# The last FFN round by thirds of the tokens

## What is computed

```python
def _conv_ffn(h, conv_prev, P):
    u = h @ P['ffn_w_up']                       # 1024 -> 5632
    ext = jnp.concatenate([conv_prev.astype(u.dtype), u], axis=1)
    z = P['ffn_conv_b']
    for j in range(CONV_WIDTH):                 # 3 taps over the tokens
        z = z + ext[:, j:j + T] * P['ffn_conv_w'][j]
    za, zb = jnp.split(z, 2, axis=-1)
    return (jax.nn.silu(za) * zb) @ P['ffn_w_down'], ext[:, T:]
...
    ff, conv_T = _conv_ffn(h2, conv0, P)
    x = x + g2 * _rmsnorm(ff, P['norm_post_ffn'])
```

## Time and profile before

| | us |
|---|---|
| median of 3 runs (lowest, highest) | 1694.37 (1692.67, 1698.76) |
| the profiled execution: its time | 1695.05 |
| the profiled execution: its span, first to last instruction | 1693.2 |
| busy in the span: TensorE matmul, VectorE, ScalarE, GpSimd | 1476.3, 827.7, 534.2, 112.1 |

### The profile page before, as it was taken

The page is one execution under the profiler, slowest core; times in us unless marked ns, Lnnn a source line. Parts: engine busy times, 40 slices in busy tenths (PEclk is TensorE's granted clock), DMA queues, the critical chain, the costliest instruction groups (busy, mean ns, idle before and its releaser), DMA issues.

```text
span 1693.2 us, 28608 instructions
## 1 busy us (share of the span) xinstructions
PE 1476.3 (87%) x12458; PEld 1377.8 (81%) x12458; DVE 827.7 (49%) x985; ACT 534.2 (32%) x677; POOL 112.1 (7%) x172
## 2 busy tenths in 40 slices
PE   4799998776688997679839999999999999999972
PEld 1799998543587897459728999999999999999972
DVE  3742333663566557361086544545455444554446
ACT  3311211555345532242244232322312313223232
POOL 0000000000202110022221000000000000000013
PEclk7899999887799999789979999999999999999987
DMA  8341111541000000212121111111111111111022
GB/s 337 106 113 51 51 38 53 176 149 51 1 3 3 3 12 26 77 38 113 38 112 54 43 63 37 50 38 46 52 37 50 51 48 50 37 37 62 25 110 100
DMA packets 30994, 107.52 MB, mean 64 GB/s; under 512 B 5352, under 2 KB 8184, under 8 KB 29872
## 3 DMA queue, kind: packets, MB, share of 16 engines
q1 hardware_dynamic: 30912, 106.30, 18.0%
HBM read 93.29 MB, written 11.40 MB: 62 GB/s over the span
## 4 chain that ended last, share of the span: by engine, by line
PE 76%; DVE 14%; ACT 5%; DMA 2%; issue 2%; SPq 1%; DVEq 0%; POOL 0%; ACTq 0%
PE ps L496 47%; PE ps L900 12%; PE ps L646 6%; DMA raw<-ada 2%; PE ps L477 2%; DVE Z L1831 2%; PE ps L628 1%; PE ps L543 1%; PE ps L558 1%; PE ps L750 1%; PE ps L748 1%; PE ps L572 1%; DVE acc L1865 1%; PE ps L769 1%; SPq L336 1%
## 5 line engine op out<-in xcount | busy, mean ns | idle before, releaser
L496 PE MATMUL ps<-XS,spl 128*128 128x344 f32 x5184 | 824.1, 321 | 38.2 <-DVE XS L1794 20.7
L496 PEld LDWEIGHTS ps<-XS,spl 128*128 128x128 f32 x5184 | 819.5, 189 | 41.8 <-issue 25.2
L900 PE MATMUL ps<-act,spl 128*128 128x344 f32 x1584 | 255.8, 322 | 9.8 <-DVE act L1843 9.0
L900 PEld LDWEIGHTS ps<-act,spl 128*128 128x128 f32 x1584 | 251.7, 190 | 12.6 <-issue 9.3
L1831 DVE SCALAR_TENSOR_TENSOR Z<-U,par,Z 128x1023 f32<-128x1023 f32 x88 | 112.9, 1283 | 162.1 <-ACT Z L1249 156.5
L1865 DVE TENSOR_TENSOR acc<-acc,ps 128x1032 f32<-128x1032 f32 x88 | 108.2, 1229 | 128.6 <-PE ps L900 128.5
L1231 ACT ACTIVATE spl<-raw 128x1024 fp32r<-128x1024 f32 x66 | 68.4, 1054 | 284.1 <-PE ps L900 198.4
L1422 DVE TENSOR_TENSOR spl<-raw,spl 128x1024 fp32r<-128x1024 f32 x28 | 34.2, 1225 | 169.6 <-ACT spl L972 169.5
L1784 DVE TENSOR_TENSOR spl<-raw,spl 128x1024 fp32r<-128x1024 f32 x66 | 79.6, 1222 | 61.3 <-ACT spl L1231 60.1
L972 ACT ACTIVATE spl<-raw 128x1024 fp32r<-128x1024 f32 x28 | 29.6, 1060 | 210.8 <-PE ps L496 210.8
L1246 ACT ACTIVATE U<-ps 128x1032 f32<-128x1032 f32 x44 | 45.3, 1029 | 160.2 <-PE ps L496 158.5
(11 more groups left out here) (280 smaller groups left out, 1568.8 us busy)
## 6 DMA issues: line engine op xcount, KB each, us to landing
raw<-ada SPq DMA_DIRECT2D x48, 512.0 KB, 5.1
raw<-up SPq DMA_DIRECT2D x44, 512.0 KB, 3.3
raw<-down SPq DMA_DIRECT2D x22, 512.0 KB, 3.4
raw<-w_in SPq DMA_DIRECT2D x20, 512.0 KB, 3.4
xT<-xT SPq DMA_DIRECT2D x4, 1032.0 KB, 11.5
X<-xT SPq DMA_DIRECT2D x1, 4128.0 KB, 13.0
x_dram<-X SPq DMA_DIRECT2D x8, 516.0 KB, 2.6
X<-x_dram SPq DMA_DIRECT2D x1, 4128.0 KB, 12.7
```

The costliest lines, as they stand in the source:

```text
L496: mm = nc.tensor.matmul(ps[:, 3 * bank_set + t, 0:SL], w[:, a, k * P:(k + 1) * P], x[:, k, b, t * SL:(t + 1) * SL], start=(k == order[0] a ...
L900: mm = nc.tensor.matmul(ps[:, 3 * (down_set(i, y)) + t, 0:SL], w[:, a, k * P:(k + 1) * P], act2[:, f, b, t * SL:(t + 1) * SL], start=(f == ...
```

## The change

The last round of the FFN is taken apart along the tokens, in three thirds of 344.

- TensorE: round 10 is written out after a loop over nine. Its last up product is made third by third, each with all 24 matmuls into a bank of its own. The last round's down products go by third t and chunk k, six matmuls each (`TAIL`, 24 products) into the banks 0 to 3 in turn. The total of the squares of a third (`tail_total`, two matmuls) stands behind product (t + 1, 3), the last at the end.
- ScalarE: Silu of the first half at once, then for each third two evacuations and the high part; then a square for each product, and `tail_root(t)` behind the square of product (t + 1, 3) or at the end. The root stays in PSUM (banks 6 and 7).
- VectorE: taps, gate and low part for the three thirds one after the other, then an add for each product. Scaling, gate and residual are two operations for a chunk of a third (`tail_norm`): the first multiplies acc by gate and root into PSUM, the second adds X1. Those of the first third stand behind the adds (1, 5) to (2, 4), the first three of the second behind (2, 5) to (2, 7), the others at the end. GpSimd scales nothing any more and sums the squares of each third.
- SP: a third of X1 is loaded into a buffer of its own ahead of the loop over the rounds, the other two where all of X1 was loaded; 24 stores of a third of a chunk replace 8 of a chunk.

```diff
+(X1a,), at2 = place([("X1a", [P, KD, SL], F32)], at2)
...
+THIRDS = [slice(t * SL, t * SL + SL) for t in range(3)]
+TAIL = [(t, k) for t in range(3) for k in range(KD)]
+def tail_square(n):
+    return (Z, U)[n % 12 // 6][:, n % 6 // 3, THIRDS[n % 3]]
...
+sp.wait_ge(s("x1_out"), 16 * KD)
+dma(X1a[:], x1_dram[:, :, THIRDS[0]], s("x1a_in"))
...
-sp.wait_ge(s("x1_out"), 16 * KD)
 sp.wait_ge(s("ffn_mm"), JOBS - KD)
-dma(X1[:], x1_dram, s("x1_in"))
+dma(X1[:, :, THIRDS[1]], x1_dram[:, :, THIRDS[1]], s("x1b_in"))
+dma(X1[:, :, THIRDS[2]], x1_dram[:, :, THIRDS[2]], s("x1c_in"))
...
-for k in range(KD):
-    sp.wait_ge(s("y_ready"), k + 1)
-    dma(io["o_y"][:, k], acc[:, k], s("y_out"))
-sp.wait_ge(s("y_out"), 16 * KD)
+for n, (t, k) in enumerate(TAIL):
+    sp.wait_ge(s("y_ready"), n + 1)
+    dma(io["o_y"][:, k, THIRDS[t]], acc[:, k, THIRDS[t]], s("y_out"))
+sp.wait_ge(s("y_out"), 16 * len(TAIL))
...
+round_of(LAST - 1)
+pe.wait_ge(s("w3_lo"), (LAST - 1) * 6 + 4)
+pe.wait_ge(s("up_out"), (LAST - 1) * 4 + 2)
+for t in range(3):
+    for k in range(KD):
+        for n, (a, b) in enumerate(((0, 0), (0, 1), (1, 0))):
+            mm = nc.tensor.matmul(ps[:, 3 + t, 0:SL], spl3[:, 0, a, k * P:(k + 1) * P], XS[:, k, b, THIRDS[t]],
+                                  start=(k == 0 and n == 0), stop=(k == KD - 1 and n == 2))
+    if t < 2:
+        mm.then_inc(s("up_third"), 1)
+mm.then_inc(s("ffn_mm"), 1)
+def tail_total(t):
+    pe.wait_ge(s("sq_added"), (KD - 1) * (t + 2))
+    if t == 2:
+        pe.wait_ge(s("y_ready"), KD)
+    nc.tensor.matmul(ps[:, 6 + t % 2, 0:SL], ones, sqF[:, THIRDS[t]], start=True, stop=False)
+    pe.wait_ge(s("sq_c"), 2 * KD + KD * (t + 1))
+    nc.tensor.matmul(ps[:, 6 + t % 2, 0:SL], ones, tail_square(KD * t + KD - 1), start=False, stop=True
+                     ).then_inc(s("sq_total"), 1)
+pe.wait_ge(s("w3_lo"), 3 * FC)
+pe.wait_ge(s("g_lo"), FC - 1)
+for n, (t, k) in enumerate(TAIL):
+    if n >= 4:
+        pe.wait_ge(s("tail_out"), n - 3)
+    elif n == 3:
+        pe.wait_ge(s("third_out"), 1)
+    else:
+        pe.wait_ge(s("up_out"), 4 * LAST - 1)
+    for f in range(2):
+        if k == 0 and f == 1:
+            pe.wait_ge(s("lo_third"), t + 1)
+        for m, (a, b) in enumerate(((0, 0), (0, 1), (1, 0))):
+            mm = nc.tensor.matmul(ps[:, n % 4, 0:SL], spl3[:, 1 + f, a, k * P:(k + 1) * P], act2[:, f, b, THIRDS[t]],
+                                  start=(f == 0 and m == 0), stop=(f == 1 and m == 2))
+    mm.then_inc(s("tail_mm"), 1)
+    if t >= 1 and k == 3:
+        tail_total(t - 1)
+tail_total(2)
...
+act.wait_ge(s("conv_done"), 2 * FC - 1)
+nc.scalar.activation(Z[:, 0], Z[:, 0], ACT.Silu).then_inc(s("silu_done"), 1)
+act.wait_ge(s("g_done"), FC)
+for t in range(3):
+    if t < 2:
+        act.wait_ge(s("up_third"), t + 1)
+    else:
+        act.wait_ge(s("ffn_mm"), JOBS - KD)
+    nc.scalar.activation(U[:, 1, THIRDS[t]], ps[:, 3 + t, 0:SL], ACT.Copy)
+    nc.scalar.activation(Z[:, 1, THIRDS[t]], ps[:, 3 + t, 0:SL], ACT.Identity,
+                         bias=col(PARAM_AT["ffn_conv_b"][0], 2 * FC - 1),
+                         scale=col(PARAM_AT["ffn_conv_w"][0] + 2 * 2 * FC, 2 * FC - 1)).then_inc(s("third_out"), 1)
+    act.wait_ge(s("g_third"), t + 1)
+    nc.scalar.activation(act2[:, 1, 0, THIRDS[t]], G[:, THIRDS[t]], ACT.Copy).then_inc(s("hi_third"), 1)
+def tail_root(t):
+    act.wait_ge(s("sq_total"), t + 2)
+    inverse_root(ps[:, 6 + t % 2, 0:SL], ps[:, 6 + t % 2, 0:SL], eps[:, 0:1], 1.0 / D).then_inc(s("std2"), 1)
+for n, (t, k) in enumerate(TAIL):
+    act.wait_ge(s("tail_out"), n + 1)
+    if n >= 12:
+        t0, k0 = TAIL[n - 12]
+        if k0 < KD - 1:
+            act.wait_ge(s("sq_added"), (KD - 1) * (t0 + 1) + k0 + 1)
+        else:
+            act.wait_ge(s("sq_total"), t0 + 2)
+    nc.scalar.activation(tail_square(n), acc[:, k, THIRDS[t]], ACT.Square).then_inc(s("sq_c"), 1)
+    if t >= 1 and k == 3:
+        tail_root(t - 1)
+tail_root(2)
...
+def tail_sum(t, k):
+    total = sqF[:, THIRDS[t]]
+    pool.wait_ge(s("sq_c"), 2 * KD + KD * t + k + 1)
+    if k == 0:
+        nc.gpsimd.tensor_copy(total, tail_square(KD * t)).then_inc(s("sq_added"), 1)
+    else:
+        pool.wait_ge(s("sq_added"), (KD - 1) * (t + 1) + k)
+        nc.gpsimd.tensor_tensor(total, total, tail_square(KD * t + k), ALU.add).then_inc(s("sq_added"), 1)
+for t, k in TAIL:
+    if k < KD - 1:
+        tail_sum(t, k)
...
-add_down(FC // 2, True)
-dve.wait_ge(s("std2"), 3)
-dve.wait_ge(s("x1_in"), 16)
-dve.wait_ge(s("down_out"), KD * (FC // 2))
-out, x1 = acc[:, :, T:N], X1[:, :, T:N]
...
+z, u = Z[:, 1], U[:, 1]
+for t in range(3):
+    dve.wait_ge(s("third_out"), t + 1)
+    for n in (1, 0):
+        d = CW - 1 - n
+        a, b = max(t * SL, d), min(t * SL + SL, T)
+        link(nc.vector.scalar_tensor_tensor(z[:, a:b], u[:, a - d:b - d],
+                                            col(PARAM_AT["ffn_conv_w"][0] + n * 2 * FC, 2 * FC - 1), z[:, a:b],
+                                            ALU.mult, ALU.add))
+    if t == 2:
+        link(nc.vector.tensor_copy(at_chunk(ftail, 2 * FC - 1), u[:, T - 2:N]))
+        nc.vector.tensor_tensor(z[:, T:N], z[:, T:N], at_chunk(conv_add, 2 * FC - 1), ALU.add
+                                ).then_inc(s("conv_done"), 1)
+        dve.wait_ge(s("conv_done"), 2 * FC)
+    dve.wait_ge(s("silu_done"), FC)
+    nc.vector.tensor_tensor(G[:, THIRDS[t]], Z[:, 0, THIRDS[t]], z[:, THIRDS[t]], ALU.mult).then_inc(s("g_third"), 1)
+    dve.wait_ge(s("hi_third"), t + 1)
+    nc.vector.tensor_tensor(act2[:, 1, 1, THIRDS[t]], G[:, THIRDS[t]], act2[:, 1, 0, THIRDS[t]].bitcast(F32),
+                            ALU.subtract).then_inc(s("lo_third"), 1)
+def tail_add(t, k):
+    n = KD * t + k
+    y = acc[:, k, THIRDS[t]]
+    dve.wait_ge(s("tail_mm"), n + 1)
+    nc.vector.tensor_tensor(y, ps[:, n % 4, 0:SL], y, ALU.add).then_inc(s("tail_out"), 1)
+def x1_of(t):
+    return X1a[:] if t == 0 else X1[:, :, THIRDS[t]]
+def tail_samples():
+    out, x1 = acc[:, :, T:N], X1[:, :, T:N]
+    link(nc.vector.tensor_tensor(out, out, over_rows(ps[:, 6, 0:SL], T - 2 * SL, SL), ALU.mult))
+    link(nc.vector.tensor_tensor(out, out, gate[:, 1, :, 1:9], ALU.mult))
+    link(nc.vector.tensor_tensor(out, out, x1, ALU.add))
+def tail_norm(t, k):
+    w = min(SL, T - t * SL)
+    y = acc[:, k, t * SL:t * SL + w]
+    if k == 0:
+        dve.wait_ge(s("std2"), 3 + t)
+        dve.wait_ge(s(("x1a_in", "x1b_in", "x1c_in")[t]), 16)
+        if t == 2:
+            tail_samples()
+        elif t == 0:
+            dve.wait_ge(s("third_out"), 3)
+    scaled = ps[:, 4 + k % 2, 0:w]
+    link(nc.vector.scalar_tensor_tensor(scaled, y, gate[:, 1, k, 0:1], ps[:, 6 + t % 2, 0:w], ALU.mult, ALU.mult))
+    nc.vector.tensor_tensor(y, scaled, x1_of(t)[:, k, 0:w], ALU.add).then_inc(s("y_ready"), 1)
+for t in range(3):
+    for k in range(KD):
+        tail_add(t, k)
+        if t == 1 and k >= 5:
+            tail_norm(0, k - 5)
+        elif t == 2 and k < 5:
+            tail_norm(0, k + 3)
+        elif t == 2:
+            tail_norm(1, k - 5)
+for k in range(3, KD):
+    tail_norm(1, k)
 for k in range(KD):
-    if k < POOL_FROM:
-        link(nc.vector.tensor_tensor(acc[:, k, 0:T], acc[:, k, 0:T], G[:, 0:T], ALU.mult))
-    else:
-        dve.wait_ge(s("scaled"), 2 * (KD - POOL_FROM) + k - POOL_FROM + 1)
-    nc.vector.scalar_tensor_tensor(acc[:, k, 0:T], acc[:, k, 0:T], gate[:, 1, k, 0:1], X1[:, k, 0:T], ALU.mult,
-                                   ALU.add).then_inc(s("y_ready"), 1)
+    tail_norm(2, k)
```

More of the change, by code:

```diff
@@ L176, in build_program @@
         (raw3, spl3), at2 = place([("raw3", [P, 3, D], F32), ("spl3", [P, 3, 2, D], F32R)], RING)
+        (X1a,), at2 = place([("X1a", [P, KD, SL], F32)], at2)
+        assert at2 <= end - base
         (X1,), _ = place([("X1", [P, KD, N], F32)], REM)
@@ L891, in down @@
                     elif y == 2:
-                        pe.wait_ge(s("up_out"), up2(i))
+                        pe.wait_ge(s("up_out"), i * 4 + 1)
                     else:
                         pe.wait_ge(s("down_out"), i * 8 + (y - 10))
-                    first = down_slot(i)
                     for f in range(2):
-                        w = spl3[:, (first + f) % 3]
+                        w = spl3[:, (2 + f) % 3]
                         for n, (a, b) in enumerate(((0, 0), (0, 1), (1, 0))):
                             for t in range(3):
-                                mm = nc.tensor.matmul(ps[:, 3 * (down_set(i, y)) + t, 0:SL], w[:, a, k * P:(k + 1) * P],
+                                mm = nc.tensor.matmul(ps[:, 3 * (y % 2) + t, 0:SL], w[:, a, k * P:(k + 1) * P],
                                                       act2[:, f, b, t * SL:(t + 1) * SL],
@@ L905, in _ @@
             LAST = FC // 2
[L907 to L917, removed]
             for m in range(4):
@@ L924, in _, with round_of @@
                         ).then_inc(s("ffn_mm"), 1)
```

(20 more changed lines are left out.)

11 lines of the change are left out of this document (2 added, 9 removed).

## The result

The changed kernel takes 1677.47 us (median of 4 runs, 1676.29 to 1679.94), the kernel before 1693.53 (median of 4, 1692.67 to 1698.76). The ratio is 0.9902, with an interval of 0.9887 to 0.9917: 16.1 us less, where 1678 us and 16.8 us less in the span were forecast.

The account below looks back on a forecast made before the run. TensorE bounds the kernel until 1623.5 us; behind that, four steps in a row, with VectorE the new bound. The span falls 16.8 us, from 1693.2 to 1676.4; taken from the median 1677.6, forecast 1678 us, range 1674 to 1687.

Parts of the forecast that it names:

- VectorE's stretch: From the first root at 1641.5 VectorE is the bound; its work and waits sum to 31.05 us, ending at 1672.5.
- the clock at 1.00 between 1624 and 1650: Sign expected in the trace after: TensorE's granted clock stays at 1.00 during the last down products.
- half clock: Rival: TensorE's 2.2 us stall and lower duty bring its clock to 0.5 in the last products; 1688 us, chance 0.10.
- The write to PSUM: Term for writing 24 scaled chunks to PSUM and reading them back: 0.05 us each, 1.2 us, moving 1672.5 to 1673.7.
- The stores: Term behind VectorE's last operation: last stores of 172 KB land in 1.85 us, 2.65 us remain to the span's end.
- The third root: Stands at 1661.2 while VectorE has second-third chunks until 1663.5, so costs nothing; without that cover up to 3.4 us.
- VectorE busy nearly throughout from 1629: Sign expected in the trace after: VectorE works nearly without pause from 1629 to 1673.7 us.
- The early load of X1: A third of X1 ahead of two weight loads on SP's queue takes 4.2 us, covered by 22 us: costs nothing.
- The waits for the roots: VectorE waits 1.4 us for the first root and 1.2 us for the second.
- The shared port: Rival: eight GpSimd sums after 1641.5 each hold VectorE for 0.93 us, 7.4 us in all; 1685 us, chance 0.12.
- The detour through PSUM: Rival: PSUM write and dependent read cost more per scaled chunk; at 1.2 us a chunk 1705 us, chance 0.06.
- The loads drain: Rival: ScalarE runs empty before each table load for the roots, 5.1 us more on the path; 1683 us, chance 0.02.

Follow-up runs that it names:

- light: Changed kernel with one of three parts (low weights by high activations) left out of last-round down products from product 12 on; 1677.40 us, ratio 0.9907.
- share: Changed kernel with GpSimd adding X1 to six of the 24 chunks, whose scaled values VectorE writes to SBUF; 1677.07 us, ratio 0.9898.
- fill: Changed kernel with TensorE's pause behind product 3 filled by 13 matmuls whose result nobody reads; 1675.95 us, ratio 0.9897.
- sbuf: Changed kernel with the scaled value written to SBUF instead of PSUM; 1678.20 us, ratio 0.9909.
- best: Changed kernel with share's edit, plus VectorE adding the first four down products between the gating steps; 1672.72 us, ratio 0.9881.

## Why the prediction was right, step by step

Taking the 2.1 us off that the execution after is earlier, the steps as forecast (first number) and as measured:

| step | forecast - 2.1 | measured |
|---|---|---|
| thirds gated and split | 1620.2, 1623.3, 1626.9 | 1620.1, 1623.3, 1626.9 |
| TensorE's pause | 2.2 | 2.15 |
| first twelve products done | 1634.9 | 1636.7 |
| first root | 1639.4 | 1641.4 |
| second root | 1652.1 | 1654.4 |
| third root | 1659.1 | 1662.9 |
| VectorE through with the second third | 1661.4 | 1663.6 |
| last operation of VectorE | 1671.6 | 1672.6 |
| end of span | 1674.3 | 1674.8 |

The bound was forecast rightly: VectorE's stretch from the first root on, which *light* and *share* show to be what sets the end. That the end is off by only 0.5 us is in part luck: three errors nearly cancel, and 0.1 of VectorE's stretch is left:

- **The clock, +2.0 up to the first root.** The step "the clock at 1.00 between 1624 and 1650" failed. The pause itself was forecast to 0.05 us, but not that the clock falls behind it: the 48 matmuls took 9.38 us instead of 7.54, which is 1.84. Of this *fill* shows 1.56 to be the clock's and leaves 0.28 of start and end of the run, which 0.157 us a matmul does not hold. The last 0.2 is a slip of the sum: for the first root its own terms give 1641.7 instead of 1641.5, and from the add of product 19 to the second root they give 4.1 us (0.5, two loads of 1.28, 0.53 and 0.48) where 3.8 were put; the rows have 4.1 (1650.26 to 1654.37). A clock of 0.5 in the products stood among the prediction's own signs of being wrong. It came, 0.61 and 0.54 over two windows of 2 us, and was too short to leave the range. The rival *half clock* had the mechanism, but not its course: it kept the clock down through the last 20 products, where the rows show it back at 1.00 from 1632 to the last product. The two stretches held against it show that a pause does not always bring the clock down; they could not show that this one would not. The row that was nearer, the mean of 0.91 over the 25.1 us behind the stall, stood on the rival's side and got too little weight. Its 144 matmuls are 22.6 us at 0.157 and took 25.1: 2.5 us, as a term of the sum, would have been nearer to the 1.84 than nothing was.
- **The write to PSUM, -1.2.** This term of the sum was mis-sized: 0.05 us for each of 24 chunks were put on, between -0.03 and 0.17, and the measured price is none (*sbuf*: 0.564 and 0.569). VectorE's stretch, from the first scaling at 1641.41 to 1672.58, took 31.17 us; 31.05 without that term and 32.25 with it had been worked out. The choice nearest to the reads would have been zero.
- **The stores, -0.4.** From VectorE's last operation to the end it took 2.2 us instead of 2.65. The median store landed in 1.8 us, as was worked out (1.85); the 0.8 taken from the end of the kernel before, for what lies beside the transfer, was too much.

The DMA rows after, which answer to the earlier trace rows:

```profile
o_y<-acc SPq DMA_DIRECT2D x24, 172.0 KB, 1.8
X<-x_dram SPq DMA_DIRECT2D x2, 1376.0 KB, 8.4
X1a<-x_dram SPq DMA_DIRECT2D x1, 1376.0 KB, 7.1
```

The rest, point by point:

- **The third root** was right in its effect and close to wrong. It was to come 2.3 us before VectorE needs it and came 0.7 before. TensorE had done nothing for 6.39 us, and the four matmuls of its total took 1.52 and 1.35 us at a granted clock of 0.50 instead of 0.74 twice. In *share* and *best*, where VectorE is faster, this cover is gone and 0.39 us are on the path.
- **VectorE busy nearly throughout from 1629** did not hold. Up to the first root it waits for products and works 4.7 of 12.4 us (1629.0 to 1641.4), as an add of 0.51 for each product of 0.94 had to give; from there to the last product it works 9.85 of 10.1.
- **The early load of X1** cost nothing, as said (TensorE's work in the rounds stays unbroken, and the weight tile behind it is first read 22 us after the start of the rounds, as before); a third landed in 7.1 us rather than the 4.2 worked out, still well inside its 22 us.
- **The waits for the roots**: VectorE waits 1.09 and 1.23 us, where 1.4 and 1.2 had been put.
- **The shared port** is no rival for the kernel as it is: the scaling with its column from SBUF takes 0.561 to 0.581 us in all 24 places, beside GpSimd's sums or not. *sbuf* shows that the contention is real for two SBUF tiles, so that the detour through PSUM is what keeps it away.
- **The detour through PSUM** as a loss is excluded by the same rows.
- **The loads drain**: the logarithm starts 0.02 us after its load ends (1639.08 and 1639.10), the exponential 0.01, and each load follows at most 0.02 us behind the operation before it. The Trainium skill (ScalarE: Activation LUTs, What ACT_TABLE_LOAD costs) puts 1.38 us of draining beside every load; no such time is in these rows.

## What to carry to other kernels

When a last step is cut into pieces so that it runs behind the product before it, the gain is what the next bound leaves: here 16.3 of the some 45 us that TensorE did not need, because VectorE's 31 us took over at the first root. Write down for each engine which operation it must do last before the first piece can end, and put what gives buffers back (the adds that free PSUM banks) ahead of work that nobody waits for yet: four adds moved forward were worth 3.4 us here. A short pause in front of a dense run of products can cost more than its length: here 2.15 us of pause, and 1.56 more in the products behind it, by the clock that fell.

## What the runs showed of the hardware

- A pause of 2.15 us after over 700 us of nearly unbroken products was followed by a granted clock of 0.61 and 0.54 over two windows of 2 us, and the 48 matmuls behind it took 1.84 us longer than at 0.157 us each; 13 matmuls whose result nobody reads, put into the pause, gave 1.56 of it back. Elsewhere TensorE was busy for only 0.87 of 2 us and the clock stayed at 1.00. What decides between the two was not settled.
- VectorE's scaling of a third takes 0.569 us into PSUM and 0.564 into SBUF (medians of 24), and the dependent add takes 0.51 to 0.52 from either when nothing holds it up: PSUM is a place for an intermediate value that keeps the add from having two SBUF inputs.
- Where VectorE's add has two SBUF inputs and meets a GpSimd sum, either engine can lose: 1.13 us instead of 0.52 for VectorE's add, 1.21 instead of 0.925 for GpSimd's sum, by which of them had begun.
